# Sparse attention: the causal mask is added by VectorE in PSUM instead of by TensorE products

## The reference, cut to what matters

```python
m_s = (tok <= tq[:, None, None]) ...
s_s = jnp.einsum('bqghd,bqgkld->bghqkl', qb, k_sel) ... * scale
p_s = masked_softmax(s_s, m_s)
...
m_w = (tk[None, :] <= tq[:, None]) & (tq[:, None] - tk[None, :] < WINDOW) & (tk[None, :] >= 0)
s_w = jnp.einsum('bqghd,bkgd->bghqk', qb, kwb) * scale
p_w = masked_softmax(s_w, m_w)
```

## Time and profile before

| what | value |
|---|---|
| time, three runs | 749.19, 750.99, 750.94 us; median 750.94 us |
| profiled execution, span from the first to the last instruction | 750.2 us |
| busy share of the span | TensorE 94%, VectorE 63%, ScalarE 55%, GpSimd 16% |
| layer 0 attention, sparse units | about 102 to 161 us of the span |

### The profile page before, as it was taken

One profiled execution on the slowest core, in us unless ns is written; L12 is line 12 of the kernel. 1 busy time (PEld: TensorE's weight loads), 2 busy tenths in 40 slices (PEclk: granted clock), 3 DMA queues, 4 the chain that ended last, 5 costly groups with the idle time before them and its releaser, 6 DMA issues.

```text
span 750.2 us, 15402 instructions
## 1 busy us (share of the span) xinstructions
PE 707.4 (94%) x6629; PEld 615.4 (82%) x6629; DVE 471.0 (63%) x664; ACT 414.7 (55%) x674; POOL 118.5 (16%) x163
## 2 busy tenths in 40 slices
PE   4999998899999999999999998988899999999996
PEld 3789965678888888888889888987688888888885
DVE  3778787656866756544666878553567756756423
ACT  5744876647755555532798746533258555555311
POOL 8111066700000000000250077500000000000000
PEclk9999999999999999999999999999999999999999
DMA  9946710007656555554755340000047556555511
GB/s 303 328 144 199 280 57 2 1 1 253 224 169 201 192 172 206 183 192 145 235 173 169 114 163 9 4 5 4 3 141 252 196 169 199 194 173 209 180 57 56
DMA packets 78277, 111.71 MB, mean 149 GB/s; under 512 B 2124, under 2 KB 64738, under 8 KB 78210
## 3 DMA queue, kind: packets, MB, share of 16 engines
q1 hardware_dynamic: 77090, 107.67, 43.1%
q0 software_dynamic: 976, 3.04, 1.3%
q10 hardware_dynamic: 144, 0.04, 0.0%
HBM read 109.68 MB, written 1.05 MB: 148 GB/s over the span
## 4 chain that ended last, share of the span: by engine, by line
PE 81%; ACT 8%; DVE 7%; issue 3%; DMA 1%; DVEq 0%; SPq 0%; ACTq 0%
PE ps L1038 20%; PE ps L733 12%; PE ps L735 11%; PE ps L734 11%; PE ps L1041 10%; PE ps L1203 5%; PE ps L1213 4%; ACT w_hi L1400 3%; DVE w_lo L1867 2%; PE ps L893 1%; PE ps L844 1%; DMA hn<-mem 1%; PE ps L867 1%; ACT scores L1452 1%; DVE row_max L1938 1%
## 5 line engine op out<-in xcount | busy, mean ns | idle before, releaser
L1867 DVE TENSOR_TENSOR w_lo<-w_raw,w_hi 128x2048 fp32r<-128x2048 f32 (+2 forms) x101 | 227.5, 2266 | 101.4 <-ACT w_hi L1400 101.3
L1400 ACT ACTIVATE w_hi<-w_raw 128x2048 fp32r<-128x2048 f32 (+2 forms) x101 | 189.1, 1892 | 46.7 <-PE ps L735 45.2
L1038 PE MATMUL ps<-x_hi_lo,w_hi 128*128 128x512 f32 x640 | 201.2, 396 | 0.0
L1041 PEld LDWEIGHTS ps<-x_hi_lo,w_lo 128*128 128x128 f32 x640 | 120.2, 188 | 28.4
L1041 PE MATMUL ps<-x_hi_lo,w_lo 128*128 128x256 f32 x640 | 125.7, 278 | 0.0
L1038 PEld LDWEIGHTS ps<-x_hi_lo,w_hi 128*128 128x128 f32 x640 | 97.4, 189 | 0.0
L733 PE MATMUL ps<-w_hi,x_hi_lo 128*128 128x512 f32 (+3 forms) x240 | 83.1, 346 | 6.3 <-DVE x_hi_lo L2087 4.4
L734 PE MATMUL ps<-w_lo,x_hi_lo 128*128 128x512 f32 (+3 forms) x240 | 81.0, 338 | 0.0
L735 PE MATMUL ps<-w_hi,x_hi_lo 128*128 128x512 f32 (+3 forms) x240 | 81.0, 337 | 0.0
L733 PE MATMUL ps<-w_hi,hidden_hi 128*128 128x512 f32 x176 | 68.6, 390 | 0.0
L734 PE MATMUL ps<-w_lo,hidden_hi 128*128 128x512 f32 x176 | 68.5, 389 | 0.0
(11 more groups left out here) (367 smaller groups left out, 1079.8 us busy)
## 6 DMA issues: line engine op xcount, KB each, us to landing
w_raw<-w_ffn_in SPq DMA_DIRECT2D x44, 1024.0 KB, 5.1
w_raw<-w_ffn_out SPq DMA_DIRECT2D x22, 1024.0 KB, 5.0
w_raw<-rwkv_w_in SPq DMA_DIRECT2D x11, 1024.0 KB, 5.4
w_raw<-w_out SPq DMA_DIRECT2D x8, 1024.0 KB, 4.9
w_raw<-nsa_w_in SPq DMA_DIRECT2D x6, 1024.0 KB, 15.1
w_raw<-w_mem_kv SPq DMA_DIRECT2D x2, 1024.0 KB, 8.9
w_raw<-nsa_cmp_k_w SPq DMA_DIRECT2D x2, 1024.0 KB, 5.5
w_raw<-nsa_cmp_v_w SPq DMA_DIRECT2D x2, 1024.0 KB, 5.4
```

The source lines that it names most:

```text
L1038: pe.matmul(psum[:, bank + j, :], kt_of(w_hi, i, k)[:, cols[j]], xx[:, k, :, :].rearrange("p c n -> p (c n)"), start=k == 0, stop=False)
L1041: ins = pe.matmul(psum[:, bank + j, 0:SEQ], kt_of(w_lo, i, k)[:, cols[j]], xh[:, k, :], start=False, stop=k == KD - 1)
L1400: act.activation(w_hi[:, i % SPL, 0:size(i)], raw[:, i % RAW, 0:size(i)], ACT.Copy).then_inc(hi_done, 1)
L1867: dve.tensor_tensor(w_lo[:, i % RAW, 0:size(i)], raw[:, i % RAW, 0:size(i)], w_hi[:, i % SPL, 0:size(i)], ALU.subtract).then_inc(lo_done, 1)
```

## The change

VectorE adds the mask to the own columns of the four score blocks of a sparse unit, in place in PSUM, with one instruction ahead of the reduction (new L1936). The two mask products per unit are no longer issued, and the last product of the scores now closes the accumulation and releases VectorE. Memory units (`nbr` = 1) are as before, in both layers. GpSimd still makes the rounded copies of the mask and of the identity, which nothing reads now.

```diff
                             lhs, rhs = mqT[r, f - FT, tile(t)], mkT[r, f - FT, :]
                         ins = pe.matmul(psum[:, SC_BANK[u % 2][e], b * SEQ:b * SEQ + nk * P], lhs, rhs, start=b == 0,
-                                        stop=kind == "mem")
-                if kind == "nsa":
-                    for e in range(2):
-                        own = psum[:, SC_BANK[u % 2][e], :].rearrange("p (b n) -> p b n", b=2)[:, :, tile(t)]
-                        ins = pe.matmul(own, ident_r[:], cmask_r[:], start=False, stop=True)
+                                        stop=b == nbr - 1)
                 ins.then_inc(a_sc, 1)
...
                 src = psum[:, bank:bank + 2, :].rearrange("p e (b n) -> p (e b) n", b=2) if nbr == 2 else psum[:, bank:bank + 2, :]
+                if nbr == 2:
+                    own = src[:, :, tile(UNITS[layer][i][1])]
+                    link(dve.tensor_tensor(own, own, cmask[:, P:].unsqueeze(1).to_broadcast([P, n, P]), ALU.add))
                 link(dve.tensor_reduce(mx[:, u % SLOTS, 0:n], src[:, :, 0:nk * P], AX.X, ALU.max))
```

## The result

The changed kernel is slower: 755.47 us in the median of six runs (752.88 to 758.13) against 751.03 us for the kernel before on the same chips. The ratio is 1.0055 with a 95% interval of 1.0029 to 1.008, so 2.2 to 6.0 us more, 4.1 in the middle (4.4 by the medians). The forecast was 2.3 us more. The median of 755.47 us lies at the upper edge of the stated range (751.4 to 755.5 us) and above the forecast's own (752.3 to 754.2 us). Three later timed runs of 889, 1327 and 1784 us, far outside all others, are left out of the medians and counts of this text.

What follows compares the result with a forecast made beforehand. Layer 0's sparse attention was taken as bound by a loop through TensorE, VectorE and ScalarE; 0.89 us at units 4 and 5 plus 1.40 over five hops gave 2.3 us more, 753.2 us, 8-in-10 range 751.4 to 755.5.

Steps and rivals of the forecast that it cites:

- The price of the add: Sparse attention of layer 0, each sparse unit: VectorE's 512-element mask add takes 0.71 us, wait for its write included.
- slow-write rival: VectorE's add writing PSUM would be 0.55 us longer, seven times on the path: 3.8 us more, 757.0 us; chance 10%.
- GpSimd beside the add: Attention of layer 0: GpSimd's products running beside VectorE's add do not hold it up; cost put at nothing.
- one slow negation: Unit 5, before the change: VectorE's negation took 0.38 us against a median 0.17, ending when GpSimd's two products did.
- When the add starts: Sparse units: without mask products, VectorE's work follows 0.05 us after the end of the scores.
- The start: Units 4 and 5: maxima of unit 5 1.11 us late, its exponentials and the scores of unit 7 0.89 us late.
- rival in which the start does not count: Scores of unit 7 keep their place through slack in another wait; only later units pay, 752.3 us; chance 15%.
- The hops: Units 7, 9, 11, 13 and 15: maxima gain 0.43 and lose 0.71 us, 0.28 later each, 1.40 us in all.
- VectorE's other work fits into its waits: Attention steps: ScalarE's and VectorE's other work has waits of 0.57 to 1.48 us around it, which take the rest.
- reaches the end whole: After the attention TensorE is busy 26.78 of 26.80 us, so any delay in leaving the attention arrives whole at the end.
- Nothing else moves: Whole kernel: beyond the 2.3 us, memory units are untouched, no transfer depends on the change, GpSimd keeps its work.
- GpSimd rival: Units 7, 11, 13 and 15: the add waits for GpSimd products, 4 x 0.46 = 1.8 us more, 755.0 us; chance 10%.

Runs made afterwards that it cites:

- fillers: Changed kernel plus two matmul products per sparse unit, read by nobody, in TensorE's waits; ratios 1.0046 and 1.0032, medians 754.0 and 753.56 us.

## Why the prediction was right in sign and place, and short in size

The third profile of the changed kernel has the same 3.4 us low stretch near 100 us as the kernel before and none later, and its span is 752.7 us, 2.5 over 750.2. So it can be laid beside the steps of the forecast.

```profile
102.96 0.81 PE L844 MATMUL ps<-kT,qT 64*128 64x128 f32 x8
...
105.68 0.69 DVE L1936 TENSOR_TENSOR ps<-ps,causal_mask 128x512 f32<-128x512 f32 x1
...
107.87 0.69 DVE L1936 TENSOR_TENSOR ps<-ps,causal_mask 128x512 f32<-128x512 f32 x1
...
108.60 0.69 DVE L1937 TENSOR_REDUCE row_max<-ps 128x4 f32<-128x512 f32 x1
...
112.77 0.71 PE L844 MATMUL ps<-kT,qT 64*128 64x128 f32 x8
113.49 0.28 DVE L1982 TENSOR_TENSOR x_hi_lo<-ps,x_hi_lo 128x128 fp32r<-128x128 f32 x1
113.69 0.69 DVE L1936 TENSOR_TENSOR ps<-ps,causal_mask 128x512 f32<-128x512 f32 x1
...
132.21 1.13 PE L844 MATMUL ps<-kT,qT 64*128 64x256 f32 x8
133.39 0.70 DVE L1936 TENSOR_TENSOR ps<-ps,causal_mask 128x512 f32<-128x512 f32 x1
134.12 1.22 DVE L1937 TENSOR_REDUCE row_max<-ps 128x4 f32<-128x1024 f32 x1
...
146.70 1.06 PE L863 MATMUL ps<-ident,scores 128*128 128x128 f32 x8 [1.50 <-ACT probsT L1465]
```

- **The price of the add.** Said: 0.71 us, 0.69 for the instruction and the wait behind it. Measured: 690 to 700 ns in all twelve, and 0.73 from its start to the reduction's. A destination in PSUM costs next to nothing extra (691 ns into SBUF). The slow-write rival falls.
- **GpSimd beside the add.** Said: no contention. The longest of the twelve adds is 700 ns in every profile with the whole add, and in this one GpSimd was at work during eleven of them. That rival falls too. The Trainium skill, "SBUF — State Buffer", section "Who interferes with whom", says that a VectorE instruction with at most one SBUF input, outside the two-port modes, does not contend with GpSimd. The trace agrees, with those 700 ns. The forecast knew of one slow negation, 384 ns; the trace before has three in sparse units (384, 320 and 252 ns), and in this profile none there is over 190.
- **When the add starts.** Said: 0.05 after the end of the scores. In unit 13 the scores start at 132.21, take 1.13, and the add starts at 133.39.
- **The start.** From the scores of unit 4 to the maxima of unit 5 were 4.59 us and are 5.64, 1.05 more (said: 1.11). To the scores of unit 7 were 8.97 and are 9.81, 0.84 more (said: 0.89). The rival in which the start does not count falls.
- **The hops.** From the scores of unit 7 to the transposes of unit 13 were 32.33 us and are 33.93, 1.60 more (said: 1.40). Of the 0.20 that the forecast lacks, 0.16 lie at unit 7: its scores end at 113.48, but VectorE still works on L1982 from 113.49, and the add starts at 113.69 instead of 113.53. The sentence that VectorE's other work fits into its waits failed there. Four hops by the ruler cost 1.15 us (29.32 less 28.17), 0.29 each (said: 0.28).
- **The way to the end.** 0.84 + 1.60 = 2.4 us arise in the attention and the span is 2.5 longer, but the near agreement is partly chance: the scores of unit 4 were already 0.64 late (102.96 for 102.32), so 3.08 us leave the attention, and a part of it comes back in the recurrence of layer 1. The forecast's "reaches the end whole" is exact up to that stage; behind it, it holds only on average over runs. Before, the maxima of a memory unit in front of that stage started at 434.84 and a row behind it at 547.33; here they are 3.10 and 2.50 later, in the first profile of the changed kernel 4.51 and 3.02 (439.35 and 550.35). First the row before, then the two of this profile:

```profile
547.33 0.58 ACT L1534 ACTIVATE ps<-ps 128x512 f32<-128x512 f32 x1
```

```profile
437.94 0.69 DVE L1937 TENSOR_REDUCE row_max<-ps 128x2 f32<-128x512 f32 x1 [0.55 <-PE ps L844]
...
549.83 0.58 ACT L1530 ACTIVATE ps<-ps 128x512 f32<-128x512 f32 x1
```

That the loop's 2.4 us reach the time is shown by the timed runs: at clocks of 0.993 or more the changed kernel's median is 2.4 us over the kernel before.

The waits tell the same from the other side (engine and line, waited for, us in total, times, longest). Before:

```profile
PE ps L867 <- ACT probsT L1469: 4.2, 5, 1.5
```

In this profile:

```profile
PE ps L863 <- ACT probsT L1465: 9.3, 9, 1.8
...
DVE ps L1936 <- PE ps L844: 3.2, 6, 0.9
```

VectorE waits 3.2 us for scores where it waited 8.8, and TensorE waits 9.3 us for ScalarE's copies where it waited 4.2, so the wait has changed sides.

**What the sum lacked** is a term: "Nothing else moves". The granted clock moved. I had read it at 1.00 in the windows of rows 2 and taken it for a constant. The forecast's mechanism was right and the loop's 2.4 us are its 2.3; that the whole result of 4.1 to 4.4 us still lies inside the stated range, at 755.47 us of 755.5, is luck: its upper end takes in the GpSimd rival's 755.0 us and some scatter, and neither rival nor term stood for the clock.

Two profiles at the upper level, the first and the third of the changed kernel, show what TensorE did: in 121 to 146 us it was busy 18.7 to 19.0 us of 25 instead of 21.5. In the third it waited before the transposes of each of the units 3 to 13, up to 1.79 us, where the kernel before had such waits at six of these eleven, up to 1.48. The Trainium skill, "TensorE: Matmul & The Clock Gate", Part 1, says that a hardware block sets the clock by how busy TensorE has been. The counts agree: TensorE is less busy and the low level (0.50) comes more often.

That the excess over the loop is the clock is shown within the changed kernel. Its 13 runs at a mean clock of 0.990 or less take 757.1 us, its six at 0.993 or more 753.3. And in the traces, from the scores of unit 4 to the transposes of unit 13 are 41.30 us before and 43.74, 45.41 and 47.91 in the third, first and second profile of the changed kernel, of which about 0.2, 8.4 and 13.6 us were at the lower level.

That a less busy TensorE is the reason for the lower clock rests on the fillers. They leave the ruler as it is, and with them the low clock became rare (1 run of 23 instead of 13 of 21; on one chip 0 of 12 instead of 4 of 6), while the time fell from 755.6 to 753.6 us on that chip. The 95% intervals of those two ratios overlap (1.0037 to 1.0086, and 1.0013 to 1.0052), so the count of low clocks is the firmer evidence. The kernel without mask points the same way: 750.5 us at 0.9925, and 748.7 at 0.995 with fillers, on two chips and with overlapping intervals. Loop 2.4 and clock some 2 make the 4 to 5 that were measured.

Open is how much the two halves of the change share in it. Taking work off TensorE (no mask) and making it wait longer (add and products) went with median clocks of 0.9925 and 0.992, where the kernel before had 0.994 to 0.995. The kernel with half of the add is about 1 us slower than its loop and a clock loss of 2 us would make it; its clock, 0.9875, was lower than the 0.990 of the changed kernel on another chip, and no run tells why.

## What to carry to other kernels

Where engines hand work round in a loop, count what an edit puts between two hand-overs and multiply by the hops; an operation that is cheap in total (8.5 us of VectorE time in 750) costs what it adds to each hop, here 0.71 - 0.43 us. The better place for such work was the wait of the engine that already had it: the same mask products, issued one step earlier, made the kernel 1.5 to 1.6 us faster than the kernel before (ratios 0.9977 and 0.9984, the first clear of no change, the second just not), and faster than the changed kernel, without touching VectorE. And an edit that takes work from TensorE in a stage where it already waits is to be priced with the clock that it may lose: look at the granted clock of several runs, not of one profile.

## What the runs showed of the hardware that I had not expected

The granted clock of one kernel varies from run to run, and with it the time: 0.983 to 0.997 and 752.6 to 760.6 us for the changed kernel, 748.0 to 756.8 us for the kernel before. Three profiles of the changed kernel gave spans of 752.7, 753.3 and 758.9 us. Matmuls that nobody reads, in TensorE's waits, made low clocks rare and the kernel some 2 us faster. And the recurrence of layer 1, which the change does not touch, took 108.6 to 112.5 us between the same two rows in three profiles at the upper clock.
